# Gathering U four units ahead of V in a product-key expert layer, with the query weights in 512-column chunks

## The reference, cut to what matters

```python
q = (h @ w_query).reshape(B, S, 8, 2, 128)              # w_query: 2048 x 2048
s = einsum('bshcd,hckd->bshck', q, sub_keys)            # 2 x 128 scores per head and token
top_s, top_i = top_k(s, 16)                             # per half
best_s, best_i = top_k(top_s[..0, :, None] + top_s[..1, None, :], 16)   # of 256 sums
eid = i1 * 128 + i2                                     # 16 of 16384 experts
g = softmax(best_s)
a = gelu(einsum('td,thkd->thk', h, expert_u[eid]))      # 128 picks per token
out = einsum('thk,thkd->td', g * a, expert_v[eid])
x = layernorm(ALPHA * h + out)
```

## Time and profile before

| | |
|---|---|
| median of 3 runs | 1940.51 us (1935.63 to 1942.42) |
| profiled execution | 1937.93 us |
| its span, first to last instruction | 1936.2 us |
| PE busy | 1523.6 us, 79% |
| VectorE busy | 1074.2 us, 55% |
| ScalarE busy | 406.8 us, 21% |
| POOL busy | 706.8 us, 37% |
| gathers' DMA queue | 556.83 MB, 69.7% of 16 engines' span |
| other loads (the hardware queue of SP and ScalarE) | 85.99 MB, 14.1% |

### The profile page before, as it was taken

One profiled execution on the slowest core, in us unless ns is written; L12 is line 12 of the kernel. 1 busy time (PEld: TensorE's weight loads), 2 busy tenths in 40 slices (PEclk: granted clock), 3 DMA queues, 4 the chain that ended last, 5 costly groups with the idle time before them and its releaser, 6 DMA issues.

```text
span 1936.2 us, 17261 instructions
## 1 busy us (share of the span) xinstructions
PE 1523.6 (79%) x6198; PEld 914.3 (47%) x6198; DVE 1074.2 (55%) x1713; ACT 406.8 (21%) x851; POOL 706.8 (37%) x564
## 2 busy tenths in 40 slices
PE   6999999999974937777777777777597777767796
PEld 5679989989963822222222222222242322222242
DVE  3665655655676076646556465564755646544444
ACT  3655465464300021101011010110101101010000
POOL 1100000000154068455455454555375454455331
PEclk8899999999987969999999999999799999999999
DMA  9545445446289369999999999999999999999995
GB/s 309 206 148 160 132 133 172 131 162 229 88 343 405 99 265 422 421 422 421 422 422 421 421 422 421 422 421 421 410 422 421 421 421 422 422 422 422 421 422 231
DMA packets 173045, 644.64 MB, mean 333 GB/s; under 512 B 13342, under 2 KB 100518, under 8 KB 106920
## 3 DMA queue, kind: packets, MB, share of 16 engines
q0 software_dynamic: 78640, 556.83, 69.7%
q1 hardware_dynamic: 90976, 85.99, 14.1%
q10 hardware_dynamic: 3352, 0.80, 0.2%
HBM read 641.47 MB, written 2.10 MB: 332 GB/s over the span
## 4 chain that ended last, share of the span: by engine, by line
DMA 51%; PE 35%; POOL 5%; DVE 3%; issue 3%; SPq 1%; ACT 1%; ACTq 1%; DVEq 1%; POOLq 0%
DMA v_slot<-in_expert_v_dram,eid 47%; PE psum_all L429 17%; PE psum_all L687 7%; PE psum_all L637 5%; POOL u_slot L376 3%; POOL v_slot L391 2%; DMA w_ring<-in_w_query_dram 2%; DMA u_slot<-in_expert_u_dram,eid 2%; SPq L264 1%; PE psum_all L543 1%; PE psum_all L479 1%; PE psum_all L480 1%; PE psum_all L481 1%; DVE u_slot L1296 1%; DVE w_lo L969 1%
## 5 line engine op out<-in xcount | busy, mean ns | idle before, releaser
L687 PE MATMUL psum_all<-v_slot,diag 128*128 128x512 f32 x1968 | 911.4, 609 | 324.3 <-DMA v_slot<-in_expert_v_dram,eid 299.7
L1296 DVE SCALAR_TENSOR_TENSOR u_slot<-u_slot,xh 128x2048 f32<-128x2048 f32 x256 | 583.3, 2290 | 488.3 <-DMA u_slot<-in_expert_u_dram,eid 488.0
L687 PEld LDWEIGHTS psum_all<-v_slot,diag 128*128 128x128 f32 x1968 | 359.9, 191 | 875.2 <-issue 451.3
L391 POOL DMA_INDIRECT v_slot<-in_expert_v_dram,eid x256 | 375.1, 1465 | 444.2 <-PE psum_all L687 411.3
L376 POOL DMA_INDIRECT u_slot<-in_expert_u_dram,eid x256 | 304.3, 1188 | 248.8 <-DVE u_slot L1296 163.7
L969 DVE TENSOR_TENSOR w_lo<-w_ring,w_hi 128x512 fp32r<-128x512 f32 x240 | 161.6, 690 | 126.9 <-ACT w_hi L720 124.4
L429 PE MATMUL psum_all<-act_hi,w_hi 128*128 128x256 f32 x640 | 185.6, 290 | 17.0 <-DVE w_lo L969 13.9
L429 PE MATMUL psum_all<-act_lo,w_hi 128*128 128x256 f32 x640 | 182.4, 285 | 0.0
L429 PE MATMUL psum_all<-act_hi,w_lo 128*128 128x256 f32 x640 | 182.2, 285 | 0.0
L720 ACT ACTIVATE w_hi<-w_ring 128x512 fp32r<-128x512 f32 x240 | 148.8, 628 | 144.0 <-PE psum_all L429 143.7
L905 ACT ACTIVATE u_act<-u_dot 128x16 f32<-128x16 f32 x16 | 3.5, 216 | 742.1 <-DVE u_slot L1296 742.1
(11 more groups left out here) (217 smaller groups left out, 1130.5 us busy)
## 6 DMA issues: line engine op xcount, KB each, us to landing
w_ring<-in_w_in_dram SPq DMA_DIRECT2D x88, 512.0 KB, 4.6
w_ring<-in_w_out_dram SPq DMA_DIRECT2D x32, 512.0 KB, 4.4
w_ring<-in_w_query_dram SPq DMA_DIRECT2D x32, 512.0 KB, 4.6
w_ring<-in_cmp_k_w_dram POOLq DMA_DIRECT2D x8, 1024.0 KB, 7.1
w_ring<-in_cmp_v_w_dram POOLq DMA_DIRECT2D x8, 1024.0 KB, 5.7
u_slot<-in_expert_u_dram,eid POOLq DMA_INDIRECT x256, 36.3
v_slot<-in_expert_v_dram,eid POOLq DMA_INDIRECT x256, 35.7
xh<-in_x_dram SPq DMA_DIRECT2D x4, 512.0 KB, 7.2
```

The costliest lines, as they stand in the source:

```text
L391: nc.gpsimd.indirect_dma_start(out=v_slot[m % RV][:, :], out_offset=None, in_=expert_v[0], in_offset=bass.IndirectOffsetOnAxis(ap=eid[:, n ...
L687: ins = nc.tensor.matmul(bank[4 + q][:, :], diag[:, n % 2, k, :], v_slot[m % RV][:, 512 * q:512 * q + 512], start=m % (TOPK * PH) == 0, st ...
L1296: V.scalar_tensor_tensor(u_slot[m % RU][:, :], u_slot[m % RU][:, :], 1.0, xh[:, n // PH, :], ALU.mult, ALU.mult, accum_out=u_dot[:, n, k:k ...
```

## The change

- POOL sends U of four units (64 gathers) ahead of the first V, then twelve U to fourteen V, so that U is two units ahead at its end, as before. V's first gather, not its third, waits for the last query matmul.
- `w_query` comes in four chunks of 512 columns (two heads), each in four quarters of the rows, in 2 KB rows, into two rings of four quarters. The second ring lies where `mix_hi` and `mix_lo` were, on two V slots and the diagonals.
- ScalarE does the exponentials and the Gelu of units 0 to 2 behind the scores of heads 3 to 5, and later ones in step with V; VectorE's gates come behind the eleventh dot of the next unit, not the third.
- Head 0 has its two query halves in banks 0 and 1, and both are done for the first tokens while `h` is transposed (through six banks) ahead of the second tokens. Head 1 waits for both evictions.
- The second tokens' token-major `h` moves from POOL to VectorE, behind the ids of unit 0; the norm rows lie on other U slots, and the seventh U gather waits for that.
- The second half's sum uses banks 0 to 3; PE no longer waits for the first half's take, which moves from unit 10 to unit 11.

```diff
-LAG = 2
+AHEAD = 4
+BEHIND = 2
...
+    ln_g = at("ln_g", [P, D], F32, oc + 80 * K)
+    ln_b = at("ln_b", [P, D], F32, oc + 88 * K)
+    wq_ring = [at(f"wq_ring{i}", [P, 4, 4, 512], F32, (o_ring, oc + 32 * K)[i]) for i in range(2)]
...
+        def load_wq(j, q):
+            for n in range(2):
+                sp.dma_start(wq_ring[j % 2][:, q, 2 * n:2 * n + 2, :],
+                             wq_v[:, 4 * q + 2 * n:4 * q + 2 * n + 2, 512 * j:512 * j + 512]
+                             ).then_inc((s_w, s_wb)[j % 2][q], 16)
+        for q in range(4):
+            sp.wait_ge(S["lo_done"], S_Q + 4 * (q - 3))
+            load_wq(0, q)
+        sp.wait_ge(S["slot_used"], S_Q)
+        for q in range(4):
+            load_wq(1, q)
+        for j in range(2, 4):
+            for q in range(4):
+                sp.wait_ge(S["wq_used"], 4 * (j - 2) + q + 1)
+                load_wq(j, q)
...
-        pool.wait_ge(S["xt_mm"], 8)
-        nc.gpsimd.tensor_tensor(xh[:, 1, :], xh[:, 1, :], ln_g[:, :], ALU.mult)
-        nc.gpsimd.tensor_tensor(xh[:, 1, :], xh[:, 1, :], ln_b[:, :], ALU.add)
...
+            if m == 6:
+                pool.wait_ge(S["h1_ok"], 1)
...
-            if m == 2:
-                pool.wait_ge(S["wq_used"], 2 * PH)
+            if m == 0:
+                pool.wait_ge(S["wq_used"], 16)
...
+        for m in range(TOPK * AHEAD):
+            gather_u(m // TOPK, m % TOPK)
+        sent = TOPK * AHEAD
+        for m in range(TOPK * NU):
+            while sent < min(TOPK * NU, TOPK * AHEAD + (m + 1) * (NU - AHEAD) // (NU - BEHIND)):
+                gather_u(sent // TOPK, sent % TOPK)
+                sent += 1
+            gather_v(m // TOPK, m % TOPK)
...
+        def head0_unit(u):
+            pe.wait_ge(S[("hT_act", "hT_dve")[u % 2]], u // 2 + 1)
+            for k in (2 * u, 2 * u + 1):
+                for c in range(2):
+                    query_mm(0, c, k, bank[c][:, 0:128], 0, 1)
+        pe.wait_ge(S["lncol_ok"], 1)
+        pe.wait_ge(S["sk_ok"], 4)
         pe.wait_ge(S["acc_dve"], 2 + 4 * NG + 8)
-        for u in range(8):
+        for u in range(6):
             transpose_h(u)
+        head0_unit(0)
+        transpose_h(6)
+        head0_unit(1)
+        transpose_h(7)
+        for u in range(2, 8):
+            head0_unit(u)
         scores_of(0, 0, 0, 1, 1)
+        for c in range(2):
+            for k in range(KC):
+                query_mm(0, c, k, bank[c][:, 128:256], 1, 2)
         for h in range(1, PH):
             b = (h - 1) % 2
-            if h > 1:
-                pe.wait_ge(S["qp_ok"], h)
+            pe.wait_ge(S["qp_ok"], max(h, 2))
...
-                if m == TOPK * PH:
-                    pe.wait_ge(S["acc_taken"], 1)
...
-                    ins = nc.tensor.matmul(bank[4 + q][:, :], diag[:, n % 2, k, :],
+                    ins = nc.tensor.matmul(bank[(4 if n < PH else 0) + q][:, :], diag[:, n % 2, k, :],
...
         for h in range(1, PH):
+            query_out(h, (h - 1) % 2)
+            score_out(h, (h - 1) % 2, 0, 2, h + 2)
+            if 3 <= h <= 5:
+                expo_gate(h - 3)
+                gelu_unit(h - 3)
         act.wait_ge(S["eps2_ok"], 1)
+        done = 3
         for n in range(NU):
-            if 1 < n + 1 < NU:
-                expo_gate(n + 1)
-            gelu_unit(n)
+            while done < min(NU, max(n + 1, AHEAD + (6 * n - 7) // 7)):
+                expo_gate(done)
+                gelu_unit(done)
+                done += 1
             diagonals(n)
...
         ids(0)
+        token_major(1)
+        dve.drain().then_inc(S["h1_ok"], 1)
         for n in range(NU):
             for k in range(TOPK):
                 dot(n, k)
-                if k == 2 and n:
-                    gates_of(n - 1)
                 if k == 1 and n + 1 < NU:
                     ids(n + 1)
-                if k == 4 and n == PH + LAG:
+                if k == 2 and n == 11:
                     take(0)
+                if k == 10 and n:
+                    gates_of(n - 1)
```

More of the change, by code:

```diff
@@ L236, in build @@
     s_w1 = [nc.alloc_semaphore(f"s_w1_{i}") for i in range(4)]
+    s_wb = [nc.alloc_semaphore(f"s_wb{i}") for i in range(4)]
     s_u = [nc.alloc_semaphore(f"s_u{i}") for i in range(RU)]
@@ L617, in transpose_h @@
                 pe.wait_ge(S["xn_act"], u // 2 + 1)
[L618 to L621, removed]
+            if u >= 6:
+                pe.wait_ge(S[("hT_act", "hT_dve")[u % 2]], 1)
             for kk in range(2):
@@ L624, in transpose_h, with query_mm, query_half @@
                     col = 128 * (2 * u + kk)
-                    ins = nc.tensor.transpose(bank[4 + u % 4][:, 256 * kk + 128 * t:256 * kk + 128 * t + 128],
+                    ins = nc.tensor.transpose(bank[2 + u % 6][:, 256 * kk + 128 * t:256 * kk + 128 * t + 128],
                                               xh[:, t, col:col + 128], ident[:, :])
             ins.then_inc(S["xt_mm"], 1)
[L629 to L643, removed]
+        def query_mm(h, c, k, o, t0, t1):
+            j = h // 2
+            if k % 4 == 0:
+                if j % 2:
+                    pe.wait_ge(s_wb[k // 4], 32 * (j // 2 + 1))
+                else:
+                    pe.wait_ge(s_w[k // 4], 480 + 32 * (j // 2 + 1))
+            ins = nc.tensor.matmul(o, wq_ring[j % 2][:, k // 4, k % 4, 256 * (h % 2) + 128 * c:256 * (h % 2) + 128 * c + 128],
+                                   hT[:, k, 128 * t0:128 * t1], start=(k == 0), stop=(k == KC - 1))
+            if h % 2 and c and k % 4 == 3:
+                ins.then_inc(S["wq_used"], 1)
+            if h % 2 == 0 and c and k == KC - 1:
+                ins.then_inc(S["q_mm"], 1)
+        def query_half(h, c, b):
+            for k in range(KC):
+                query_mm(h, c, k, bank[b][:, 256 * c:256 * c + 256], 0, 2)
         def scores_of(h, b, t0, t1, ready):
@@ L893, in _ @@
                 k = 2 * u + kk
-                ins = nc.scalar.activation(hT[:, k, :], bank[4 + u % 4][:, SEQ * kk:SEQ * kk + SEQ], ACT.Identity,
+                ins = nc.scalar.activation(hT[:, k, :], bank[2 + u % 6][:, SEQ * kk:SEQ * kk + SEQ], ACT.Identity,
                                            bias=lncol[:, 16 + k:17 + k], scale=lncol[:, k:k + 1])
@@ L920, in root, with query_out, query_out0 @@
                                  ).then_inc(S["std2_ok"], 1)
-        def query_out(h, b, t0, t1):
-            if h == 0 and t0 == 0:
-                act.wait_ge(S["q0_mm"], 1)
-            else:
-                act.wait_ge(S["wq_used"], 2 * h + 2)
-            nc.scalar.activation(qp[:, b, :, 128 * t0:128 * t1], bview(b, 2, SEQ)[:, :, 128 * t0:128 * t1], ACT.Copy
-                                 ).then_inc(S["qp_ok"], 1)
+        def query_out(h, b):
+            if h % 2:
+                act.wait_ge(S["wq_used"], 2 * h + 2)
+            else:
+                act.wait_ge(S["q_mm"], h // 2 + 2)
+            nc.scalar.activation(qp[:, b, :, :], bview(b, 2, SEQ), ACT.Copy).then_inc(S["qp_ok"], 1)
+        def query_out0(t):
+            act.wait_ge(S["q_mm"], t + 1)
+            for c in range(2):
+                ins = nc.scalar.activation(qp[:, t, c, 128 * t:128 * t + 128], bank[c][:, 128 * t:128 * t + 128], ACT.Copy)
+            ins.then_inc(S["qp_ok"], 1)
         def score_out(h, b, t0, t1, done):
@@ L1230, in _, with token_major @@
                 k = 2 * u + kk
-                ins = V.tensor_scalar(hT[:, k, :], bank[4 + u % 4][:, SEQ * kk:SEQ * kk + SEQ], lncol[:, k:k + 1],
+                ins = V.tensor_scalar(hT[:, k, :], bank[2 + u % 6][:, SEQ * kk:SEQ * kk + SEQ], lncol[:, k:k + 1],
                                       lncol[:, 16 + k:17 + k], ALU.mult, ALU.add)
             ins.then_inc(S["hT_dve"], 1)
+        def token_major(t):
+            V.tensor_tensor(xh[:, t, :], xh[:, t, :], ln_g[:, :], ALU.mult)
+            dve.drain()
+            V.tensor_tensor(xh[:, t, :], xh[:, t, :], ln_b[:, :], ALU.add)
+            dve.drain()
+        dve.wait_ge(S["xt_mm"], 8)
         dve.wait_ge(S["s_lnrow"], 32)
[L1235 to L1238, removed]
+        token_major(0)
         def ids(n):
@@ L1312, in take @@
                 cols = xh[:, t, 512 * q:512 * q + 512]
-                ins = V.scalar_tensor_tensor(cols, cols, 1.0 if t else ALPHA, bank[4 + q][:, :], ALU.mult, ALU.add)
-            ins.then_inc(S["acc_taken"], 1)
+                V.scalar_tensor_tensor(cols, cols, 1.0 if t else ALPHA, bank[(0 if t else 4) + q][:, :],
+                                       ALU.mult, ALU.add)
             dve.drain()
```

43 lines of the change are left out of this document (8 added, 35 removed).

## The result

The changed kernel takes 1876.93 us (median of four runs, 1875.41 to 1880.09), the kernel before 1941.24 beside it: a ratio of 0.9676 with a 95% interval of 0.9653 to 0.97. The profiled execution has a span of 1873.7 us against 1936.2, so 62.5 us less. The dense part ahead of the change differs by 2.1 us between these two executions (the first transposes start at 510.66, before at 512.78).

The account below looks back on a forecast made before the run. Gathers at full DMA rate bound the second half, so only empty DMA time before 720 us can be won: 26.2 more gathers at 2.485 us make 65, plus 1.4, some 66 off 1940.51; forecast 1872, 8-in-10 range 1855 to 1893.

Parts of the forecast that it names:

- The count: Gathers landed by 720 us, when the queue is full for good: each one more is worth 2.485 us at the end.
- Part 1: Before the gathers: POOL's passes move to VectorE, first gather issues at 536.5 instead of 543.13, some 6.5 us earlier.
- Part 2: Scores of heads 0 and 1: ids(1) comes 2 us later, at 557.8 instead of 555.84.
- Ten gathers cover 25 us: While VectorE idles for ids(1) after two dots: eight slots and two freed keep the DMA supplied for 25 us.
- Part 3: Query weights in 2 KB rows beside gathers: queues alternate by packet, weights get 90 GB/s instead of 50.
- Part 4: U four units ahead, gates between heads: removes VectorE's 73.88 us wait; 63 gathers by 720 us against 36.8, 65 us.
- Part 5: From 720 us on: separate banks for the sums remove PE's 24.6 us wait for the take, worth 1.4 us.
- The forecast's own check: Gathers by 720 us: 181 us from 539, less 6 empty and 21 for weights, make 154 us, or 62 gathers.
- Rival A: Gathers up to 720 us: better overlap, no gap, VectorE never late; 69 gathers, gain 80, 1859 us; chance 0.08.
- B: Queries hold V up: weights keep 50 GB/s, first V issues at 736; gain 50, 1890 us; chance 0.12.
- C: VectorE still stands for a gate or id behind ScalarE's queue; half of 26 gathers lost, 1906 us; chance 0.05.
- D: Gather stage slower: PE bounds it at the lower clock level, 78 us more, 1950 us; chance 0.03.

Follow-up runs that it names:

- e4: The changed kernel with the second tokens' token-major pair of passes back on POOL, beside VectorE's own pair; 1883.69 us.
- e9: The changed kernel with VectorE doing the ids of unit 1 behind the sixth dot of unit 0 instead of the second; 1878.6 us.
- e2: The changed kernel with query weights loaded in 1 KB rows instead of 2 KB, the same bytes; 1877.62 us.
- e3: The changed kernel with U sent three units ahead instead of four, nothing else; 1895.21 us.

## Why the prediction was right

It said 1872, the median is 1876.93. Its sum was 66 us; the span shrank by 62.5, and by 60.4 from the first transposes on. The 2.1 us between the two are the dense part, which happened to end earlier in the profiled execution: luck, not the change. By its steps, in the forecast's frame:

- **The count.** That the time follows from the gathers landed by 720 us holds to 1.6 us in twelve profiles, with the terms named above the table.
- **Part 1.** First gather 536.4, forecast 536.5; a pass alone 2.28 and 2.29 us, forecast 2.2. e4 shows its worth, 6.3 us (forecast 6.5).
The Trainium skill, SBUF — State Buffer, "Who interferes with whom", has a VectorE instruction with two SBUF inputs and a GpSimd instruction that reads SBUF shut each other out. By that rule e4 agrees: VectorE's pass takes 5.87 us against 2.28, and it ends 2.14 us behind POOL's.
- **Part 2.** ids(1) at 557.2, forecast 557.8. "Ten gathers cover 25 us" fell short: the tenth was issued at 551.78 us, the 11th at 566.70, and 7.6 us lie between a gather's issue and its dot (534.28 to 541.91). So the 18th dot ended at 604.9, forecast 599. But the weights took the DMA meanwhile (413 GB/s from 550 to 637), and e9 shows that it cost nothing that the runs can tell.
- **Part 3.** Packets 221 to 219; a weight packet took an engine 22.4% x 80 / 219 = 0.082 us and a pair 80 / 220 = 0.364, forecast 0.081 and 0.36. The weights got 84 GB/s, forecast 90. e2 shows that this step was not needed for the time.
- **Part 4.** No wait for a gate. Unit 1's Gelu at 647.3 (forecast 643.5), the third Gelu at 692.7 (689), the last query matmul ends at 703.7 (699.5), the first V at 722.7 (717.5). One gap, before 707, and none after 720.
- **Part 5.** 422 GB/s throughout, the take's 1.4 us as worked out, no wait of PE for it.
- **The mis-sized term** is the 63 gathers of part 4: 61.4 landed by 720 us of the trace, and 60.7 by 717.9, which is 720 in the forecast's frame. The forecast's own check had 62, for 181 us less 6 for the gap and 21 for the weights. Those 181 us are 536.9 to 717.9 of the trace, and each loss can be priced there from the windows, against 422 GB/s. The gap cost 4.4 us (20 x 101 / 422 = 4.8, less 0.4 that fall behind 717.9). The weights cost 21.8: their 8.39 MB at 422 GB/s are 19.9, and 87 x 9 / 422 = 1.9 are lost from 550 to 637, as both queues together move 413. Two losses the check had left out: 2.6 us at the start (14 x 104 / 422 = 3.5, less 0.9 ahead of 536.9), as the traffic took longer to rise than the 2.5 us allowed behind the first issue, and 20 x 23 / 422 = 1.1 from 660 to 680. Together that is 3 us more than charged, or 1.2 gathers; the step from 63 to 62 lies between the forecast's own two workings.
- **The dip from 660 to 680** is the stop for ids(3), by its timing. POOL issues nothing between 651.24 and 661.66, and the traffic falls to 354 and 392 GB/s from 665 to 675; the gap follows the stop for ids(4) (706.50) in the same way. In the changed kernel's other profile that stop ends 6.3 us later, at 667.96, and the dip lies at 670 to 680. No run moved ids(3) alone.

Rival A is out: the gap came and 69 never landed. B is out for 2 KB rows, and e2 shows it out for 1 KB too, if narrowly: the last query matmul ended 4 us ahead of the first V, helped by the dry spell. C: no gate is waited for above 0.3 us; the 6.88 us for the scores of ids(1) were forecast, and by e9 they cost nothing that the runs can tell. D: the granted clock stood at 0.98 over 720 to 1320 us with PE busy 469 of 600, and V's matmuls wait 247.2 us for the DMA.

## What to carry to other kernels

Where a queue is full from some point to the end, count what has landed by then: one number priced every edit ahead of it here. An engine's instruction order is a chain of its own: ScalarE stood 38.93 us for one Gelu ahead of an eviction, which held the last two heads back by 30 us, and how far to send ahead had to be chosen with it (three units suffice once it is moved). Before you lengthen a transfer's rows, ask whether anybody waits for it last.

## What the runs showed of the hardware

- Two DMA queues with work took turns packet by packet at both sizes tried: 246 to 246 with 1 KB rows beside 8 KB, 221 to 219 with 2 KB.
- Both together (2 KB rows) moved 413 GB/s (550 to 637 us) where the gathers alone moved 422.
- An issue of a gather on POOL took 0.94 us while VectorE stood (e3, 702.72) or worked on ids (changed kernel, 651.24), and 1.91 beside its dots, one per 2.21 us.
- The dense part ended 4.9 us apart in two profiles of the changed kernel (510.66 and 515.54).
